# Split-precision projections of a dilated attention: one 512-column pass for the high weight half

## The reference

```python
k = rope(k.reshape(bsz, s, SWA_N_GROUPS * SWA_KV_HEADS, SWA_HEAD_DIM), pos)      # shared_kv: x @ w_kv
...
proj = x @ w_in                                                                  # dilated_mixer
q, g = jnp.split(proj, [SWA_Q_TOTAL], axis=-1)
q = rope(q.reshape(bsz, s, SWA_N_GROUPS * SWA_Q_HEADS, SWA_HEAD_DIM), pos) * (SWA_HEAD_DIM ** -0.5)
...
o_g, lse_g = dilated_window_attention(q[:, :, gi], k_sh[:, :, gi], v_sh[:, :, gi], window, dilation)
...
return (o.astype(x.dtype) * jax.nn.silu(g)) @ w_out
```

## Time and profile before

| what | us |
|---|---|
| median of 3 runs | 753.12 |
| lowest, highest of the runs | 752.69, 759.79 |
| the profiled execution: its span, first to last instruction | 757.1 |
| PE busy in it | 730.8 |
| DVE, ACT, POOL busy in it | 524.7, 396.1, 104.3 |

### The profile page before, as it was taken

How to read it: one execution, slowest core, us unless ns; L and a number is a source line. 1 busy time by engine, 2 the same in 40 slices (tenths; PEclk the granted TensorE clock), 3 DMA queues, 4 the chain that set the end, 5 groups by cost and what they waited for, 6 DMA issues and landing times.

```text
span 757.1 us, 14222 instructions
## 1 busy us (share of the span) xinstructions
PE 730.8 (97%) x5964; PEld 710.5 (94%) x5964; DVE 524.7 (69%) x778; ACT 396.1 (52%) x560; POOL 104.3 (14%) x87
## 2 busy tenths in 40 slices
PE   8899999998899999999999999999999999999995
PEld 6799899898898999999999989899999999999995
DVE  4979888886977678777767556925576347555665
ACT  4286455545364544544544348528555456556551
POOL 0130000000522000000001130000004455443000
PEclk9999999999999999999999999979999999999998
DMA  8995567555363455654566544514446553343101
GB/s 343 411 356 190 203 268 274 193 204 219 113 244 146 167 200 190 213 178 161 204 261 233 205 138 148 207 66 168 167 154 223 184 206 117 116 159 112 57 1 56
DMA packets 22265, 141.13 MB, mean 186 GB/s; under 512 B 2389, under 2 KB 3029, under 8 KB 6458
## 3 DMA queue, kind: packets, MB, share of 16 engines
q1 hardware_dynamic: 21626, 137.28, 50.1%
q0 software_dynamic: 576, 2.95, 1.0%
HBM read 139.17 MB, written 1.05 MB: 185 GB/s over the span
## 4 chain that ended last, share of the span: by engine, by line
PE 70%; DVE 13%; issue 7%; ACT 5%; DMA 3%; POOL 0%; SPq 0%; DVEq 0%; ACTq 0%
PE res L1596 20%; PE res L1598 19%; PE res L1597 19%; ACT whi L639 3%; DVE wlo L1052 3%; PE pX L1803 2%; DMA shared<-in_w_ada 1%; PE pS L1783 1%; PE pX L1982 1%; DVE shared L1065 1%; DVE raw L1065 1%; DMA y<-in_w_ada 1%; ACT sq L654 1%; PE pT L1793 1%; PE pS L1644 1%
## 5 line engine op out<-in xcount | busy, mean ns | idle before, releaser
L1596 PE MATMUL res<-hhi,whi 128*128 128x256 f32 (+1 forms) x1120 | 318.9, 285 | 4.1 <-DVE wlo L1052 1.5
L1052 DVE TENSOR_TENSOR wlo<-raw,whi 128x2048 fp32r<-128x2048 f32 (+3 forms) x101 | 229.1, 2270 | 126.4 <-ACT whi L639 126.2
L1597 PE MATMUL res<-hhi,wlo 128*128 128x256 f32 (+1 forms) x1120 | 312.9, 279 | 0.0
L1598 PE MATMUL res<-hlo,whi 128*128 128x256 f32 (+1 forms) x1120 | 312.8, 279 | 0.0
L639 ACT ACTIVATE whi<-raw 128x2048 fp32r<-128x2048 f32 (+3 forms) x101 | 188.3, 1865 | 120.2 <-issue 87.1
L1596 PEld LDWEIGHTS res<-hhi,whi 128*128 128x128 f32 (+1 forms) x1120 | 209.6, 187 | 5.9 <-issue 3.4
L1597 PEld LDWEIGHTS res<-hhi,wlo 128*128 128x128 f32 (+1 forms) x1120 | 209.4, 187 | 0.4
L1598 PEld LDWEIGHTS res<-hlo,whi 128*128 128x128 f32 (+1 forms) x1120 | 209.4, 187 | 0.2
L538 POOL TENSOR_TENSOR sq<-sq,rope 128x512 f32<-128x512 f32 x18 | 39.5, 2195 | 78.5 <-ACT sq L654 78.5
L1596 PE MATMUL res<-uhi,whi 128*128 128x256 f32 x176 | 49.3, 280 | 0.0
L1597 PE MATMUL res<-uhi,wlo 128*128 128x256 f32 x176 | 49.1, 279 | 0.0
(11 more groups left out here) (334 smaller groups left out, 1211.1 us busy)
## 6 DMA issues: line engine op xcount, KB each, us to landing
raw<-in_wts SPq DMA_DIRECT2D x97, 1024.0 KB, 5.0
raw<-in_w_ada SPq DMA_DIRECT2D x16, 1024.0 KB, 5.1
shared<-in_w_ada SPq DMA_DIRECT2D x6, 1024.0 KB, 11.1
gates<-in_wts SPq DMA_DIRECT2D x4, 768.0 KB, 13.3
raw<-in_wts SPq DMA_DIRECT2D x4, 768.0 KB, 5.6
y<-in_w_ada SPq DMA_DIRECT2D x2, 1024.0 KB, 9.2
x<-in_xT SPq DMA_DIRECT2D x2, 512.0 KB, 4.7
gv<-in_ln_rows POOLq DMA_DIRECT2D x1, 1024.0 KB, 7.5
```

Source lines behind the costliest of these rows:

```text
L1052: nc.vector.tensor_tensor(lo[:, 0:b], raw[RAW_OF["w", c] % RAW][:, 0:b], hi[:, 0:b].bitcast(f32), ALU.subtract).then_inc(lo_ready, 1)
L1596: mm(out, ah, bh, start=first, stop=False)
L1597: mm(out, al, bh, start=False, stop=False)
L1598: return mm(out, ah, bl, start=False, stop=last)
```

## The change

It treats keys, queries and gate alike (`in_parts(c)`: 19 chunks; values and output projection stay).

- The activation halves lie side by side in one tile, `hh` (128 x 8 x 2 x 256); `hhi` and `hlo` become views of it.
- For each half chunk and slice there are two passes where there were three: the high weights meet both activation halves in one pass of 512 columns, and the low weights meet the high activations in a pass of 256 columns onto the first half of the bank (`side_by_side`, `fm_parts`).
- Each half chunk fills a bank of its own, so a chunk has two results. Its two parts (columns 0 to 255 and 256 to 511) are summed outside PE: ACT copies the first part into a new tile `ssum` (two buffers), DVE adds the second part from PSUM to it.
- `swap` and `rope` read `ssum`, not PSUM, and so do the tanh and the scaled copy of the gate. New semaphores: `s_copied`, `s_cos`, `s_gates`. DVE's sums are now what drains these banks.

The first `if in_parts(b)` stands in ACT's program ahead of `high(c + 2)`, the second in DVE's.

```diff
+def in_parts(c):
+    return SK <= c < SV or SWA <= c < SOUT
...
-    return 2 if c == SK - 1 else 1
+    return 2 if c == SK - 1 or in_parts(c) else 1
...
-        hhi = sb("hhi", [P, KT, T], f32r)
-        hlo = sb("hlo", [P, KT, T], f32r)
+        hh = sb("hh", [P, KT, 2, T], f32r)
+        hhi, hlo = hh[:, :, 0, :], hh[:, :, 1, :]
...
+                if in_parts(b):
+                    n = part_index(b)
+                    if n >= 2:
+                        act.wait_ge(s_cos, min(n - 1, 15))
+                    for i in range(2):
+                        ps = result(FIRST_RESULT[b] + i)
+                        nc.scalar.activation(ssum[:, n % 2, i, :], ps[:, 0:T], ACT.Copy).then_inc(s_copied, 1)
...
-                    ps = result(FIRST_RESULT[b])
+                    act.wait_ge(drained_dve, RESULT_DRAIN[FIRST_RESULT[b] + 1][1])
+                    ps = ssum[:, part_index(b) % 2, :, :].rearrange("p a b -> p (a b)")
                     if pair:
                         act.wait_ge(sg_ready, pair)
-                    nc.scalar.activation(sth[:, :], ps[:, :], ACT.Tanh, scale=0.5).then_inc(act_self, 1)
+                    nc.scalar.activation(sth[:, :], ps, ACT.Tanh, scale=0.5).then_inc(act_self, 1)
...
+                if in_parts(b):
+                    n = part_index(b)
+                    for i in range(2):
+                        dve.wait_ge(s_copied, 2 * n + i + 1)
+                        part = ssum[:, n % 2, i, :]
+                        nc.vector.tensor_tensor(part, res[(FIRST_RESULT[b] + i) % NB][:, T:2 * T], part, ALU.add
+                                                ).then_inc(drained_dve, 1)
...
+            def side_by_side(ps, ah, al, both, first, last):
+                mm(ps, ah, both.rearrange("p s t -> p (s t)"), start=first, stop=False)
+                return mm(ps[:, 0:T], al, both[:, 0, :], start=False, stop=last)
```

More of the change, by code:

```diff
@@ L87, in kt_of, with part_index @@
     return KT, 256
+def in_parts(c):
+    return SK <= c < SV or SWA <= c < SOUT
+def part_index(c):
+    return c - SK if c < SV else c - SWA + 3
 def results_of(c):
@@ L102, in drainer_of @@
         return "dve"
-    if SK <= c < SV or SWA <= c < SWA + 12 or c >= SOUT:
+    if SK <= c < SV or SWA <= c:
         return "dve"
@@ L335, in build @@
             sth = sb("sth", [P, 512], at=st)
+            ssum = sb("ssum", [P, 2, 2, T], at=st)
             dmask = sb("dmask", [P, 1024], at=st)
@@ L405, in build @@
         sg_ready, presummed = sem("sg_ready"), sem("presummed")
+        s_copied, s_cos, s_gates = sem("s_copied"), sem("s_cos"), sem("s_gates")
         d_qk, d_max, d_exp, d_norm, d_tr, d_pT, d_pv, d_of, d_hi, d_lo = (
@@ L424, in halves @@
             if c == NC - 1:
-                return (h[:, :, :].rearrange("p a b -> p (a b)") for h in (hhi, hlo))
+                return (hh[:, k:k + 4, :, :].rearrange("p a s b -> p (a s b)") for k in (0, 4))
             if c == SK - 1:
@@ L541, in sine @@
                     pool.wait_ge(sin_done, RI[c] + 1)
-                    pool.wait_ge(drained_dve, RESULT_DRAIN[FIRST_RESULT[c]][1])
+                    pool.wait_ge(s_cos, part_index(c) + 1)
                     nc.gpsimd.tensor_tensor(dst, dst, xsw, ALU.add).then_inc(roped, 1)
@@ L646, in swap @@
             def swap(c, block_rows):
-                ps = result(FIRST_RESULT[c])
                 if c > MISC:
+                    act.wait_ge(drained_dve, RESULT_DRAIN[FIRST_RESULT[c] + 1][1])
                     act.wait_ge(roped, RI[c])
+                    ps = ssum[:, part_index(c) % 2, :, :].rearrange("p a b -> p (a b)")
+                else:
+                    ps = result(FIRST_RESULT[c])
                 n = P // block_rows
@@ L997, in _ @@
                         act.wait_ge(d_gated, pair - 1)
-                    nc.scalar.activation(sgs[:, pair % 2, :, :].rearrange("p a b -> p (a b)"), ps[:, :], ACT.Copy,
-                                         scale=0.5).then_inc(drained_act, 1)
+                    nc.scalar.activation(sgs[:, pair % 2, :, :].rearrange("p a b -> p (a b)"), ps, ACT.Copy,
+                                         scale=0.5).then_inc(s_gates, 1)
                 def dil_slot(s):
@@ L1114, in rope @@
             def rope(c, dst, table):
+                if c > MISC:
+                    dve.wait_ge(drained_dve, RESULT_DRAIN[FIRST_RESULT[c] + 1][1])
+                    nc.vector.tensor_tensor(dst, ssum[:, part_index(c) % 2, :, :],
+                                            table[:, 0:1, :].to_broadcast([P, 2, T]), ALU.mult).then_inc(s_cos, 1)
+                    return
                 ps = result(FIRST_RESULT[c])
@@ L1118, in rope @@
                                         table[:, 0:1, :].to_broadcast([P, 2, T]), ALU.mult).then_inc(drained_dve, 1)
-                if c > MISC:
-                    return
                 dve.wait_ge(drained_dve, RESULT_DRAIN[FIRST_RESULT[c]][1])
@@ L1568, in _ @@
                     pair = b - SWA - 12
-                    dve.wait_ge(drained_act, RESULT_DRAIN[FIRST_RESULT[b]][1])
+                    dve.wait_ge(s_gates, pair + 1)
                     g = sgs[:, pair % 2, :, :].rearrange("p a b -> p (a b)")
@@ L1639, in fm, with fm_parts @@
                         half()
+            def side_by_side(ps, ah, al, both, first, last):
+                mm(ps, ah, both.rearrange("p s t -> p (s t)"), start=first, stop=False)
+                return mm(ps[:, 0:T], al, both[:, 0, :], start=False, stop=last)
+            def fm_parts(c, ready, slots):
+                wait_weights(c)
+                wh, wl = weights_of(c)
+                for i in range(2):
+                    ps = bank(FIRST_RESULT[c] + i)[:, :]
+                    for k in range(KT):
+                        if ready and i == 0:
+                            ready(k)
+                        last = side_by_side(ps, wh[:, k, i * P:i * P + P], wl[:, k, i * P:i * P + P], hh[:, k, :, :],
+                                            k == 0, k == KT - 1)
+                        if k == KT - 1:
+                            last.then_inc(product_done, 1)
+                        if k % 4 == 3 and 2 * i + k // 4 + 1 in slots:
+                            dilated(slots[2 * i + k // 4 + 1])
             def warm(n, of=ident, to=pS[:, 512:640]):
@@ L2045, in _ @@
                     else:
[L2046 to L2049, removed]
+                        fm_parts(c, (lambda k: pe.wait_ge(h_lo, 3 + k // 4)) if c == SK else None, SLOTS.get(c, {}))
                 else:
```

## The result

| what | before | after |
|---|---|---|
| median, us | 756.45 (4 runs, 752.69 to 760.04) | 765.61 (4 runs, 763.54 to 770.84) |
| span of the profiled execution | 757.1 | 763.8 |

The ratio of the times is 1.0153 (95% interval 1.0101 to 1.0206): the change makes the kernel slower by 8 to 16 us. A fourth run of the kernel before, of 760.04 us, moved its median from 753.12 to 756.45 us. The forecast of 756.2 us, no difference to be told, was wrong, and the time lies above its range. So I compare from the first key pass on.

What follows compares the result with a forecast made beforehand. PE, busy 97%, was taken as the bound. Other chunks 4.95 us less, query waits 0.4 and gate chunks 7.65 more gave +3.1: profiled execution 757.1 to 760.2, median 753.12 to 756.2 us; range 748.5 to 762.5.

Steps and rivals of the forecast that it cites:

- +8.6: Last gate chunks and output projection: longer waits for sums and tanh; 7.65 us more with their own shorter passes counted.
- `SWA+13`: Gate chunk with transposes 12: high half starts at 1.66 us, chunk takes 14.1 us where it was 10.84, +3.25.
- The pass, -5.9 us: All 19 changed chunks: a slice takes 334 ns, not 353, with one load gone; 304 slices save 5.9 us.
- no gain in the passes: Rival, all changed chunks: the 11 ns go with the columns, so passes save nothing; +9.0, 762.1 us; chance 0.11.
- The rule of the Trainium skill: Rival, all changed chunks: a 512-column pass takes 131 ns; -32 + 8, about 729 us; chance 0.02.
- The waits in the query chunks, +0.4 us: Query chunks with units: ACT copies and a rope slowed beside POOL make transposes 3 and 7 late, 0.2 us each.
- nothing late: Key chunks and first query chunks, without units: added copies and sums on ACT and DVE make no wait.
- The gate chain, 7.8 to 9.8 us: Gate chunks, high half to transposes: sums, tanh and scaled copy come between low half and gate product, 2.0 us more.
- The clock: Rival, gate chunks: long PE waits drop the clock to 1.2 GHz for 10.24 us, costing 5.1; 761.3 us; chance 0.08.

## Why the prediction was wrong, point by point

The forecast was -5.9, +0.4 and +8.6 (7.65 with the gate chunks' own 0.93 put back) us, +3.1 in all. Measured to `SOUT`: 0, +2.5, +7.4, +1.4 for the clock, and -0.6 for value chunks that the change doesn't touch: 10.7. The 8.6 is itself too much: in `SWA+13` and `SWA+14` the passes ahead of a wait for the transposes would have gained nothing, so less than 0.93 us was to be put back.

- **The pass, -5.9 us: the step that failed.** "Something that isn't the column stream is the longer one, and the load is what is left" was read off the half-clock passes, which show 256 columns at one a cycle. That holds at half clock only. At full clock an f32r column took 0.44 to 0.46 ns in all forms, with half a load or a full one, and 512 of them in one pass as much as in two; why it is more than the 0.417 ns of a cycle stays open. What misled was the plain f32 rows: 216 ns for a stream that I took as twice 256 columns, which no run shows, and so as the price of 512 f32r columns. The nearest row in length was of another format. The rival "no gain in the passes" named 235 ns; it was 233. I gave it 0.11. The rule of the Trainium skill ("TensorE: Matmul & The Clock Gate", Back-to-back issue gap), about 131 ns for 512 columns in a stream, isn't met by any pass here: the bf16 one took 216.6 ns.
- **The waits in the query chunks, +0.4 us, measured 2.5.** The mechanism was the right one: two SBUF inputs, and POOL keeps DVE out. The queue behind it wasn't followed to its end. I priced the transposes; but the rope's reader is POOL's sum, and its reader the scores. They had 0.05 us to spare at unit 0. One of the two rows behind the term was no case of two SBUF inputs: the normalisation (1.34 us, line 1537) reads one tile and one factor per row. Of the four that wait only unit 0 sits in the part that I had called "nothing late".
- **The gate chain, 7.8 to 9.8 us.** After, the timeline of DVE and ACT as in the earlier trace rows:

```profile
695.39 1.93 ACT L653 ACTIVATE whi<-raw 128x2048 fp32r<-128x2048 f32 x1
697.35 2.29 DVE L1077 TENSOR_TENSOR wlo<-raw,whi 128x2048 fp32r<-128x2048 f32 x1 [1.05 <-ACT whi L653]
699.56 0.75 DVE L1577 TENSOR_TENSOR ssum<-res,ssum 128x256 f32<-128x256 f32 x2
700.35 0.63 ACT L1019 ACTIVATE sth<-ssum 128x512 f32<-128x512 f32 x1 [3.03 <-DVE ssum L1577]
700.88 0.62 ACT L1023 ACTIVATE sgs<-ssum 128x512 f32<-128x512 f32 x1
701.53 0.69 DVE L1606 SCALAR_TENSOR_TENSOR sgs<-sth,sgs 128x512 f32<-128x512 f32 x1 [1.22 <-ACT sgs L1023]
702.87 0.68 DVE L1556 CUSTOM_DVE_ANT_0 dsc<-pS,dmask 128x512 f32<-128x512 f32 x1
704.64 0.49 DVE L1565 TENSOR_SCALAR dp<-dp,drec 128x512 f32<-128x512 f32 x1
```

  From the high half's start to the transposes, 695.39 to 705.18, are 9.79 us: as forecast (9.8), and in the order forecast: low half, sums, tanh, copy, gate product.
- **Step by step**, without the gain that didn't come: transposes 12 come 2.5 us later behind unit 12's scores (9.11 against 6.63), where 3.4 were forecast; transposes 12 to 14 take 3.6 us more, of which 1.4 are the clock, so 2.2, against 2.2; from there to `SOUT` 2.7 us more, against 2.7. The one miss is `SWA+13`: the high half started 0.9 us behind the chunk's start (694.48, a quarter ahead of the scores and their wait), not 1.66, since the copies weren't carried as late there. For the same reason the wait for a bank in its middle was 0.4 us of a weight load, not 0.9 us; the longest such wait came in `SWA+15`.
- **The clock** was a rival of its own (5.1 us for 10.24 us at 1.2 GHz). The waits came nearly at full length (2.59 us each, where 3 were forecast) and it did fall, behind the 2.59 us in which PE stood still, but for 3.4 us, which cost 1.4. The rival's size was wrong: it took the length of the one stretch before.
- **The range.** Two rivals came true together: no gain (+9.0) and the clock. Together they make 767 by my own prices; I had priced each alone and ended the range 0.4 us above the higher, with no room for both, nor for a wait at a place that I hadn't listed.

## What to carry to other kernels

Before counting on fewer, longer matmul passes, find out whether the present ones are bound by columns: a row at the same clock and in the same format, not one at half clock. An operand that moves from PSUM to SBUF can make a DVE operation wait for POOL; follow who reads its result, to the end, and look for readers that already come just in time. When a value needs one more step (a sum) before other engines can use it, put that step ahead of the long operation on its engine: here this order decided 7 us (8.8 to 1.6 behind unit 12's scores), and the form of the product nothing.

## What was not expected of the hardware

- f32r passes at full clock: 0.44 to 0.46 ns a column (113 to 118 ns for 256, 176 for 384, 229 to 233 for 512), bf16 0.423.
- These passes have two spacings. In the value chunks passes of 256 columns start 117.8 ns apart in one profiled execution and 113.5 in another, of the same code, and so in long stretches elsewhere: between 240 and 420 us PE began 1531 passes in the profile of before and 1578 in that of after. That is about 5.4 us there. It isn't the new tile: with the tiles of before, the version with the units ahead of the gate had 113.4 ns in the value chunks, and with the tile of after, the one with the pass cut in two had 117.8. What sets it stays open. It may be what spreads the times: of 25 runs of the kernel before that were taken together, 13 lie between 750.7 and 754.6 us and 12 between 758.0 and 760.1. But 19 others have three between such groups, and only profiled executions show the spacing. It may also be why the profile of before stood above the median, which I put down to its half-clock stretch: the changed kernel has a stretch of 10.2 us there, too, and two of 3.4 us ahead of it, and still began its first key pass 4 us sooner.
- The granted clock went to 1.2 GHz for 3.4 us within 1.2 us of the end of a PE wait of 2.6 us: at six of the ten such waits in the gate chunks, in four of the five kernels that had them. In none of the five that had only waits of 1 us or less there did it fall. The kernel with the pass cut in two had both long waits and kept 2.4 GHz; why isn't settled.
